# Turning four retention heads on VectorE in 32-partition pieces instead of on TensorE

## The reference, cut to what matters

```python
scores = jnp.einsum('bnqhd,bnkhd->bnhqk', qc, kc) * decay[None, None]
inner = jnp.einsum('bnhqk,bnkhe->bnqhe', scores, vc)
...
o = (inner + cross).reshape(B, S, H, Dh)
mu = jnp.mean(o, axis=-1, keepdims=True)
var = jnp.mean(jnp.square(o - mu), axis=-1, keepdims=True)
on = ((o - mu) * lax.rsqrt(var + EPS)).reshape(B, S, D_RET) * gn_w.astype(f32)
return (jax.nn.silu(g.astype(f32)) * on).astype(q.dtype)
...
y = jnp.concatenate([y_lru, y_ret], axis=-1)
h = h + jnp.einsum('bse,ed->bsd', y, w_out[l])
```

## Time and profile before

| what | value |
|---|---|
| three runs | 2189.8, 2192.39 and 2192.48 us, median 2192.39 us |
| the profiled execution | 2189.45 us, span 2187.5 us, so 1.95 us lie around the span |
| granted TensorE clock, mean over the span | 0.999 |
| PE busy | 2177.1 us of the span, 9870 matmuls |
| DVE busy | 1317.3 us (60%) |
| ACT busy | 1034.8 us (47%) |
| POOL busy | 154.3 us (7%) |

### The profile page before, as it was taken

One profiled execution on the slowest core, in us unless ns is written; L12 is line 12 of the kernel. 1 busy time (PEld: TensorE's weight loads), 2 busy tenths in 40 slices (PEclk: granted clock), 3 DMA queues, 4 the chain that ended last, 5 costly groups with the idle time before them and its releaser, 6 DMA issues.

```text
span 2187.5 us, 25675 instructions
## 1 busy us (share of the span) xinstructions
PE 2177.1 (100%) x9870; PEld 1807.3 (83%) x9870; DVE 1317.3 (60%) x1594; ACT 1034.8 (47%) x1257; POOL 154.3 (7%) x260
## 2 busy tenths in 40 slices
PE   9999999999999999999999999999999999999998
PEld 7888888888888888888888888888888888888887
DVE  5764656676455645546676888665555555554444
ACT  6644444444444444444545666454444444444443
POOL 0010101011000000000111100120001000100000
PEclk9999999999999999999999999999999999999999
DMA  8775656578654657668878756687777777776664
GB/s 301 224 231 175 200 164 220 183 223 249 203 157 150 213 179 227 205 205 284 264 233 288 229 180 196 202 279 219 214 211 227 215 213 213 226 224 207 193 193 154
DMA packets 229731, 468.89 MB, mean 214 GB/s; under 512 B 16632, under 2 KB 16896, under 8 KB 228736
## 3 DMA queue, kind: packets, MB, share of 16 engines
q1 hardware_dynamic: 212128, 409.00, 60.2%
q0 software_dynamic: 17056, 57.69, 8.7%
q10 hardware_dynamic: 448, 0.86, 0.1%
HBM read 439.69 MB, written 27.79 MB: 214 GB/s over the span
## 4 chain that ended last, share of the span: by engine, by line
PE 100%; DMA 0%; ACT 0%; issue 0%; DVE 0%; ACTq 0%
PE ps L1577 32%; PE ps L1579 32%; PE ps L1578 32%; PE ps L1476 1%; PE ps L1498 1%; PE ps L1445 1%; PE ps L1487 0%; PE ps L1611 0%; PE ps L1610 0%; PE ps L1609 0%; PE ps L1515 0%; PE ps L1548 0%; PE ps L1547 0%; PE ps L1629 0%; DMA vec_b<-in_vectors 0%; PE ps L1528 0%
## 5 line engine op out<-in xcount | busy, mean ns | idle before, releaser
L935 DVE TENSOR_TENSOR w_lo<-raw,w_hi 128x1024 fp32r<-128x1024 f32 (+1 forms) x776 | 931.8, 1210 | 734.6 <-ACT w_hi L607 733.6
L607 ACT ACTIVATE w_hi<-raw 128x1024 fp32r<-128x1024 f32 (+1 forms) x776 | 811.2, 1050 | 901.9 <-PE ps L1579 843.9
L1577 PE MATMUL ps<-w_hi,xT_hi 128*128 128x512 f32 x1088 | 429.8, 395 | 0.0
L1579 PE MATMUL ps<-w_hi,xT_lo 128*128 128x512 f32 x1088 | 424.2, 390 | 0.0
L1578 PE MATMUL ps<-w_lo,xT_hi 128*128 128x512 f32 x1088 | 423.6, 389 | 0.0
L1577 PE MATMUL ps<-w_hi,u2T_hi 128*128 128x512 f32 x704 | 273.9, 389 | 0.0
L1578 PE MATMUL ps<-w_lo,u2T_hi 128*128 128x512 f32 x704 | 273.9, 389 | 0.0
L1579 PE MATMUL ps<-w_hi,u2T_lo 128*128 128x512 f32 x704 | 273.9, 389 | 0.0
L1579 PEld LDWEIGHTS ps<-w_hi,xT_lo 128*128 128x128 f32 x1088 | 204.2, 188 | 43.5
L1577 PEld LDWEIGHTS ps<-w_hi,xT_hi 128*128 128x128 f32 x1088 | 204.4, 188 | 41.2 <-issue 0.6
L1578 PEld LDWEIGHTS ps<-w_lo,xT_hi 128*128 128x128 f32 x1088 | 204.5, 188 | 40.8
(11 more groups left out here) (262 smaller groups left out, 2288.6 us busy)
## 6 DMA issues: line engine op xcount, KB each, us to landing
raw<-in_w_in SPq DMA_DIRECT2D x368, 512.0 KB, 4.5
raw<-in_w_ffn_gate SPq DMA_DIRECT2D x88, 512.0 KB, 4.5
raw<-in_w_ffn_up SPq DMA_DIRECT2D x88, 512.0 KB, 4.5
raw<-in_w_ffn_down SPq DMA_DIRECT2D x88, 512.0 KB, 4.7
raw<-in_w_out SPq DMA_DIRECT2D x64, 512.0 KB, 5.8
bounce<-tmp POOLq DMA_DIRECT2D x45, 512.0 KB, 3.7
stage<-bounce POOLq DMA_DIRECT2D x140, 128.0 KB, 5.0
raw<-in_w_mem_kv SPq DMA_DIRECT2D x32, 512.0 KB, 5.5
```

The source lines that it names most:

```text
L607: nc.scalar.activation(w_hi[:, s, 0:per], raw[:, s, 0:per], ACT.Copy).then_inc(hi_ready, 1)
L935: nc.vector.tensor_tensor(w_lo[:, s, 0:per], raw[:, s, 0:per], w_hi[:, s, 0:per].bitcast(F32), ALU.subtract)\
L1577: nc.tensor.matmul(bank(2 * par + t), x_hi, w_hi[:, s, k], start=first, stop=False)
L1579: ins = nc.tensor.matmul(bank(2 * par + t), x_lo, w_hi[:, s, k], start=False, stop=last)
```

## The change

For heads 4 to 7 the two transposes on PE, with their waits, are taken out of PE's program. DVE gets a function `ret_turn` that turns `y_tok` block by block into a new SBUF buffer `y_turned` (1 KB a partition): 4 by 4 instructions, each from 32 partitions of `y_tok` to 32 partitions of `y_turned`, two blocks of 32x32 (one for each half of the tokens) in one instruction. It stands after the split of chunks 6, 9 and 12 for heads 4, 5 and 6, one chunk after the norm. For head 7 it stands behind the norm in chunk 14. `ret_hi` and `ret_lo` read `y_turned` in place of PSUM bank 5. Heads 0 to 3 stay as they were.

```diff
+        y_turned = at("y_turned", [P, S], F32, 182.5)
...
-        def ret_y_bank(n):
-
-            return 5 if n >= QUAD else 4 + n % 2
+        def ret_yT(n):
+            return y_turned[:, :] if n >= QUAD else bank(4 + n % 2, 0, S)
...
             def ret_hi(n):
                 act.wait_ge(r_yT, n + 1)
-                nc.scalar.activation(y2T_hi[:, 8 + n], bank(ret_y_bank(n), 0, S), ACT.Copy, scale=gn_half[:, n:n + 1]).then_inc(r_hi, 1)
+                nc.scalar.activation(y2T_hi[:, 8 + n], ret_yT(n), ACT.Copy, scale=gn_half[:, n:n + 1]).then_inc(r_hi, 1)
...
+            def ret_turn(n):
+
+                dve.wait_ge(r_y, n + 1)
+                dve.wait_ge(r_hi, n)
+                to = y_turned[:, :].rearrange("p (t s) -> p t s", t=NT)
+                for m in range(4):
+                    for g in range(4):
+                        ins = nc.vector.transpose(to[32 * m:32 * (m + 1), :, 32 * g:32 * (g + 1)],
+                                                  y_tok[32 * g:32 * (g + 1), :, 32 * m:32 * (m + 1)])
+                ins.then_inc(r_yT, 1)
...
-                3: [lambda: ret_decay(4)], 5: [lambda: ret_norm(4)],
-                7: [lambda: ret_decay(5), lambda: ret_lo(4)], 8: [lambda: ret_norm(5)],
-                10: [lambda: ret_decay(6), lambda: ret_lo(5)], 11: [lambda: ret_norm(6)],
-                13: [lambda: ret_decay(7), lambda: ret_lo(6)], 14: [lambda: ret_norm(7), lambda: ret_lo(7), lambda: dve.wait_ge(in_h2, 16 * NT * NG)],
+                3: [lambda: ret_decay(4)], 5: [lambda: ret_norm(4)], 6: [lambda: ret_turn(4)],
+                7: [lambda: ret_decay(5), lambda: ret_lo(4)], 8: [lambda: ret_norm(5)], 9: [lambda: ret_turn(5)],
+                10: [lambda: ret_decay(6), lambda: ret_lo(5)], 11: [lambda: ret_norm(6)], 12: [lambda: ret_turn(6)],
+                13: [lambda: ret_decay(7), lambda: ret_lo(6)], 14: [lambda: ret_norm(7), lambda: ret_turn(7), lambda: ret_lo(7), lambda: dve.wait_ge(in_h2, 16 * NT * NG)],
...
             def ret_y(n):
                 pe.wait_ge(r_y, n + 1)
-                if n >= QUAD:
-                    pe.wait_ge(r_lo, n)
-                elif n > 1:
+                if n > 1:
                     pe.wait_ge(r_lo, n - 1)
-                if n == QUAD:
-                    pe.wait_ge(tx_free[0], w.n["j0"])
-                transposes(lambda t, c: y_tok[:, t, 0:HD], ret_y_bank(n) * NW, 1).then_inc(r_yT, 1)
+                transposes(lambda t, c: y_tok[:, t, 0:HD], (4 + n % 2) * NW, 1).then_inc(r_yT, 1)
...
-                3: [lambda: ret_y(4), lambda: ret_scores(5)], 4: [lambda: ret_values(5)],
-                6: [lambda: ret_y(5), lambda: ret_scores(6)], 7: [lambda: ret_values(6)],
-                9: [lambda: ret_y(6), lambda: ret_scores(7)], 10: [lambda: ret_values(7)], 12: [lambda: ret_y(7)],
+                3: [lambda: ret_scores(5)], 4: [lambda: ret_values(5)],
+                6: [lambda: ret_scores(6)], 7: [lambda: ret_values(6)],
+                9: [lambda: ret_scores(7)], 10: [lambda: ret_values(7)],
```

More of the change, by code:

```diff
@@ L1034, in ret_norm @@
                 half, h = n // QUAD, n % QUAD
-                nc.vector.tensor_tensor(y_tok[:, :, 0:HD], y_tok[:, :, 0:HD], gr[half][:, :, h * HD:(h + 1) * HD], ALU.mult)\
-                  .then_inc(r_y, 1)
+                ins = nc.vector.tensor_tensor(y_tok[:, :, 0:HD], y_tok[:, :, 0:HD], gr[half][:, :, h * HD:(h + 1) * HD], ALU.mult)
+                ins.then_inc(r_y, 1)
+            def ret_turn(n):
[7 more added lines that the diff above has]
+                ins.then_inc(r_yT, 1)
             def ret_lo(n):
                 dve.wait_ge(r_hi, n + 1)
-                nc.vector.scalar_tensor_tensor(y2T_lo[:, 8 + n], bank(ret_y_bank(n), 0, S), gn_half[:, n:n + 1],
+                nc.vector.scalar_tensor_tensor(y2T_lo[:, 8 + n], ret_yT(n), gn_half[:, n:n + 1],
                                                y2T_hi[:, 8 + n].bitcast(F32), ALU.mult, ALU.subtract).then_inc(r_lo, 1)
```

## The result

The changed kernel takes 2201.66 us (median of 6 runs, 2201.16 to 2204.53) against 2192.2 us before: 9.5 us more, ratio 1.0051 with a 95% interval of 1.0041 to 1.0060 (the ratio as recorded; the two medians alone give 1.0043). In a second comparison it was 1.0054 (1.0040 to 1.0067). It is slower, as forecast, by somewhat more than the 7.2 us of the likeliest case and inside the range.

A forecast was written before the change was run, and what follows sets the result against it. PE bounds the kernel, so each wait for DVE counts in full. Delays of 2.8, 2.0, 2.0 and 0.45 us sum to 7.2 us, from 2192.39 to 2199.6 us; the range takes in 2194.5 and 2203.7 us.

The forecast's parts named there:

- the likeliest case: DVE's pieces run end to end and PE keeps full clock: 7.2 us slower, 2199.6 us; chance 0.62.
- a turn on PE: Removing one head's transposes from PE saves 0.22 us, four of them 0.9 us, all that the change can win.
- spacing of the pieces: On DVE, each small transpose within a turn starts 0.237 us after the last, end to end.
- 16 pieces: One head's whole turn on DVE takes 3.8 us.
- values of head 5: PE's values step waits for the decay behind head 4's turn on DVE and starts 2.8 us later.
- values of heads 6 and 7, each: PE's values steps wait for the decay behind the turns of heads 5 and 6: 2.0 us later each.
- lo of head 7 at chunk 14: The chain of norm, turn, hi and lo makes PE begin chunk 14 0.45 us later, net of the removed turn.
- falls of the clock: Rival: PE's clock halves after a wait, losing 2 us a fall; one fall makes 9.2 us in all; chance 0.14.
- What bounds, and where the turns lie: PE bounds the kernel; DVE's turns stand ahead of decays PE needs, so PE's added waits count in full.
- The tie of DVE to the late PE: For heads 5 and 6, DVE's splits follow PE's late chunks, so each delay is 2.0 us, not 2.8 us.
- the granted clock of 1.0 in the stage: Sign expected in the changed kernel's profile: PE stays at full clock where heads 4 to 7 are worked out.
- Cover for the rest: Behind chunk 14, DVE's 2.72 us of earlier idle time covers later splits, so PE is delayed no further.

The follow-up runs named there:

- second comparison: The changed kernel itself, run again with another profile, against the kernel before: 2201.97 against 2190.98 us, ratio 1.0054.
- the idle transposes: Changed kernel plus ten or eighteen unused PE transposes ahead of the values of heads 5 to 7: 2198.42 and 2198.31 us, ratios 1.0033 and 1.0036 to the kernel before.
- head 4 alone: Only head 4 turned on DVE, heads 5 to 7 on PE as in the kernel before: 2194.24 against 2190.98 us, ratio 1.0016.

## Why the prediction came out right

The steps, in us net of the removed turn:

| step | predicted | measured |
|---|---|---|
| a turn on PE | 0.22 | 0.21 to 0.22 |
| spacing of the pieces | 0.237 | 0.249 |
| 16 pieces | 3.8 | 4.0 |
| values of head 5 | 2.8 | 3.0 |
| values of heads 6 and 7, each | 2.0 | 2.06 and 2.09, clock at 1.00 |
| lo of head 7 at chunk 14 | 0.45 | 0.61, clock at 1.00 |
| sum at full clock | 7.2 | 7.8 |
| falls of the clock | none; one of 2 as a rival | two or three, 1.4 to 1.6 each |

- **What bounds, and where the turns lie:** right. PE has nothing else to wait for, the three waits are for `probsT` from the decay behind the turn, and each is DVE's lateness in full.
- **The price of a piece:** right in kind. It runs end to end in SBUF too, because the partitions change. It was too low by 0.012 us, which makes 0.2 us a turn and the 0.6 us between the sums.
- **The tie of DVE to the late PE** behind the first wait, which made the second and third delay smaller than the first: right to 0.1 us.
- **The clock:** the choice that failed. I took full clock for the likeliest, gave one fall 0.14 and said that the waits of 2.2 us speak against more. That was a term put at nothing in the sum, and the granted clock of 1.0 in the stage, which the prediction named as a sign, did not come; its wait of 0.7 us for `y2T_lo` shows only with the idle transposes, as 1.0 us. Both profiles of the changed kernel show falls behind the two waits of 2.4 us; behind the one of 3.26 us the clock fell in the second profile and not in the first. A low clock behind the first wait is what the prediction had called a sign of being wrong, so on this point the second profile refutes it. The price, 2 us, was about right, slightly high for the changed kernel and low for the one fall of 2.75 us with head 4 alone. The falls, less the 0.8 us that the one behind the last values hides at chunk 14, are the rest of the gap: from 7.8 us to the 10.0 and 11.3 us of the stage in the two profiles.
- **Cover for the rest:** right. Behind chunk 14 nothing is later than PE itself: 774.4 us to the end of the span, before and after.
- **The range:** its top had room for one fall on top of the dearest pieces. Two or three falls behind pieces near the likely price came to less than that; so the time lies inside, in part by luck.

That idle transposes give the clock back is shown; why it fell behind the wait of 3.26 us in one execution and not in another stays open.

No version here beats the kernel before by an amount that can be told. The nearest to turns that cost nothing was one instruction a turn: 0.85 us less, 0.04%.

## What to carry to other kernels

An engine with 40% of idle time can still have no room where the work is to go: add up its work for one period of that stage, with the waits inside it (here 11.6 us on DVE against 9.56 us on PE), and don't go by its busy share of the span. A wait that only moves when the order is changed is a sign of such a lack of room. Count small instructions by their number and by whether they can overlap, and ask of every wait that is put on TensorE whether the clock may fall behind it, and add that price.

## What the runs showed of the hardware that I had not expected

- The granted clock fell to 0.50 in or right behind every wait of 2.23 to 2.46 us and those of 3.03, 3.25 and 6.14 us, but with the wait of 3.26 us only in the second of two profiles. Behind the waits of 0.99 to 1.79 us it stayed at 1.00. (All without idle transposes; the length is the idle time of the weight loads.) A low stretch lasted some 3.4 us in the changed kernel and nearly 7 us with head 4 alone. It mostly slows the work that the wait has just released.
- Eighteen idle transposes of 0.12 us in waits of 3.3 and 2.5 us kept the clock at 1.00, and so did ten.
- Pieces that change their partitions are not only held back but also last longer: 0.236 against 0.194 us for the same 32 by 64 elements.
